# Running sums of the stick-breaking attention: softplus tiles of later key blocks added on VectorE, 768 ones columns a head in place of 1280

## The reference

```
z = einsum('bqhd,bshd->bhqs', qb, k) * HEAD_DIM ** -0.5
causal = pos[None, :] < t[:, None]
log_keep = where(causal, log_sigmoid(-z), 0.0)
after = cumsum(log_keep, axis=3, reverse=True) - log_keep
w = where(causal, exp(log_sigmoid(z) + after), 0.0)
out = einsum('bhqs,bshd->bqhd', w, v)
```

## Time and profile before

| | us |
|---|---|
| median of 3 runs | 1367.83 (1367.25 to 1368.55) |
| the profiled execution | 1367.21 |
| its span | 1365.5 |
| PE busy | 1264.2 (93%) |
| DVE busy | 804.4 (59%) |
| ACT busy | 437.7 (32%) |
| POOL busy | 158.8 (12%) |

### The profile page before, as it was taken

The page is one execution under the profiler, slowest core; times in us unless marked ns, Lnnn a source line. Parts: engine busy times, 40 slices in busy tenths (PEclk is TensorE's granted clock), DMA queues, the critical chain, the costliest instruction groups (busy, mean ns, idle before and its releaser), DMA issues.

```text
span 1365.5 us, 16163 instructions
## 1 busy us (share of the span) xinstructions
PE 1264.2 (93%) x6140; PEld 1026.9 (75%) x6140; DVE 804.4 (59%) x1108; ACT 437.7 (32%) x589; POOL 158.8 (12%) x172
## 2 busy tenths in 40 slices
PE   4548778899999999999999999999999999999999
PEld 4346676778888888888877988556878888888887
DVE  2988887756555555465627895775474343343442
ACT  1323214133123132141324224786243132231321
POOL 1700450220000000004200000111400000000022
PEclk9769857999999999999999999999999999999999
DMA  8234736636444444443131222000322323233211
GB/s 257 77 100 130 218 95 226 210 121 214 161 147 178 161 158 163 163 162 115 22 119 62 93 93 93 1 1 1 119 67 93 93 92 96 88 109 105 92 61 62
DMA packets 136912, 157.68 MB, mean 115 GB/s; under 512 B 24168, under 2 KB 117536, under 8 KB 136864
## 3 DMA queue, kind: packets, MB, share of 16 engines
q1 hardware_dynamic: 121808, 151.72, 34.6%
q10 hardware_dynamic: 14480, 3.74, 1.4%
q0 software_dynamic: 576, 1.57, 0.3%
HBM read 151.65 MB, written 4.19 MB: 114 GB/s over the span
## 4 chain that ended last, share of the span: by engine, by line
PE 78%; DVE 13%; DMA 4%; ACT 2%; ACTq 2%; issue 1%; POOL 0%; DVEq 0%; SPq 0%
PE psum L1536 77%; DMA ada_ring<-in_ada_w 3%; DVE ada_acc L1007 2%; DVE w_lo L1174 1%; DVE work L1191 1%; ACTq L696 1%; DVE bz L978 1%; PE psum L1540 1%; DVE h_lo L1203 1%; DVE work L978 1%; ACT w_hi L710 1%; ACT pT L930 1%; DVE s_t L978 1%; DMA u_scratch<-ub 1%; DVE bd L1148 0%
## 5 line engine op out<-in xcount | busy, mean ns | idle before, releaser
L1536 PE MATMUL psum<-h_hi,w_hi 128*128 128x512 f32 x880 | 346.9, 394 | 14.8 <-DVE w_lo L1174 8.0
L1536 PE MATMUL psum<-h_lo,w_hi 128*128 128x512 f32 x880 | 344.3, 391 | 0.0
L1536 PE MATMUL psum<-h_hi,w_lo 128*128 128x512 f32 x880 | 344.0, 391 | 0.0
L710 ACT ACTIVATE w_hi<-w_raw 128x2048 fp32r<-128x2048 f32 x92 | 174.8, 1900 | 345.9 <-PE psum L1536 309.9
L1174 DVE TENSOR_TENSOR w_lo<-w_raw,w_hi 128x2048 fp32r<-128x2048 f32 x92 | 214.0, 2326 | 107.0 <-ACT w_hi L710 106.5
L1536 PEld LDWEIGHTS psum<-h_hi,w_hi 128*128 128x128 f32 x880 | 165.5, 188 | 55.4 <-issue 14.1
L1536 PE MATMUL psum<-a_hi,w_hi 128*128 128x512 f32 x512 | 202.4, 395 | 0.0
L1536 PE MATMUL psum<-a_hi,w_lo 128*128 128x512 f32 x512 | 202.2, 395 | 0.0
L1536 PE MATMUL psum<-a_lo,w_hi 128*128 128x512 f32 x512 | 202.1, 395 | 0.0
L1536 PEld LDWEIGHTS psum<-h_hi,w_lo 128*128 128x128 f32 x880 | 165.4, 188 | 35.9
L1536 PEld LDWEIGHTS psum<-h_lo,w_hi 128*128 128x128 f32 x880 | 165.6, 188 | 34.9
(11 more groups left out here) (279 smaller groups left out, 1473.2 us busy)
## 6 DMA issues: line engine op xcount, KB each, us to landing
w_raw<-in_mlp_w SPq DMA_DIRECT2D x64, 1024.0 KB, 5.3
ada_l_ring<-in_ada_w SPq DMA_DIRECT2D x64, 384.0 KB, 6.2
ada_ring<-in_ada_w SPq DMA_DIRECT2D x40, 384.0 KB, 4.3
w_raw<-in_cd_w_in SPq DMA_DIRECT2D x14, 1024.0 KB, 5.2
ada_first<-in_ada_w SPq DMA_DIRECT2D x24, 384.0 KB, 3.8
w_raw<-in_ab_w_in SPq DMA_DIRECT2D x4, 1024.0 KB, 7.0
w_raw<-in_ab_w_out SPq DMA_DIRECT2D x4, 1024.0 KB, 7.3
w_raw<-in_cd_w_out SPq DMA_DIRECT2D x4, 1024.0 KB, 5.1
```

Of the source, the lines that this page charges most:

```text
L710: act.activation(w_hi[n % 2][:, :, 0:w], raw[n % 2][:, :, 0:w], ACT.Copy).then_inc(hi_ready, 1)
L1536: return nc.tensor.matmul(o, lhsT, rhs, start=start, stop=stop, **kw)
```

## The change

A second place for sums appears: later_a (256 columns) and later_b (128 columns). A new DVE function, later_sums, waits until POOL has masked the softplus tiles of a head and then computes with three additions of 128 columns: later_b = query block 3 of key blocks 2 and 3 added; later_a, first half = query block 2 of key blocks 1 and 2 added; later_a, second half = query block 3 of key block 1 added to later_b, for which it waits for the first addition. It raises later_ready twice a head. DVE runs it for head s - 1 at the end of score_rows(s), behind |z| of head s; for the last head directly behind softplus_sum.

stick_sums waits for later_ready as well, before its first matmul. Block j then takes a ones matmul of 128 columns from the first tile of block j + 1, and for the rest one ones matmul from later_a (256 columns, block 0) or later_b (128 columns, block 1). Ones columns: 384 + 256 + 128 = 768 a head. The order of the float32 additions changes, the sums are the same.

```diff
@@ -203,6 +203,9 @@
     z_sb.append(place("z_sb2", [P, W1], F32, offset=sumsq_at))
     sp_sb = [lay(at, f"sp_sb{i}", [P, W1]) for i in range(2)]
     pT = lay(at, "pT", [P, NB, L])
+    later_a = lay(at, "later_a", [P, 2 * P])
+    later_b = place("later_b", [P, P], F32, offset=sumsq_at + 4 * 10 * P)
+    assert sumsq_at + 4 * 11 * P <= arena
     assert at[0] <= nc.sbuf_usable_end, (at[0], nc.sbuf_usable_end)
 
     p_at = [0, P, 3 * P, 6 * P]
@@ -386,6 +389,7 @@
     z_soft = sem("z_soft")
     sp_diag = sem("sp_diag")
     sp_ready = sem("sp_ready")
+    later_ready = sem("later_ready")
     r_ps = sem("r_ps")
     r_used = sem("r_used")
     w_exp = sem("w_exp")
@@ -1446,6 +1450,18 @@
             dve.scalar_tensor_tensor(out=sp_sb[head % 2][:, :], in0=z_sb[head % 3][:, :], scalar=0.0,
                                      in1=sp_sb[head % 2][:, :], op0=ALU.max, op1=A).then_inc(sp_diag, 1)
 
+        def later_sums(head):
+
+            s_ = sp_sb[head % 2]
+            dve.wait_ge(sp_ready, NB * (head + 1))
+            last_pair = s_[:, z_at[2] + P:z_at[2] + 2 * P]
+            own(dve.tensor_tensor(later_b[:, :], last_pair, s_[:, z_at[3]:z_at[3] + P], A))
+            dve.tensor_tensor(later_a[:, 0:P], s_[:, z_at[1] + P:z_at[1] + 2 * P], s_[:, z_at[2]:z_at[2] + P], A)\
+               .then_inc(later_ready, 1)
+            settle()
+            dve.tensor_tensor(later_a[:, P:2 * P], s_[:, z_at[1] + 2 * P:z_at[1] + 3 * P], later_b[:, :], A)\
+               .then_inc(later_ready, 1)
+
         def score_rows(step):
             for n in range(NB):
                 i = NB - 1 - n
@@ -1465,6 +1481,8 @@
             dve.tensor_scalar(sp_sb[step % 2][:, :].bitcast(I32), z_sb[step % 3][:, :].bitcast(I32),
                               0x7fffffff, None, ALU.bitwise_and)\
                .then_inc(z_abs, 1)
+            if step >= 1:
+                later_sums(step - 1)
 
         def score_norms(step):
             dve.wait_ge(p_exp, NB * (step + 1))
@@ -1850,6 +1869,7 @@
         def stick_sums(pr):
             s_ = sp_sb[pr % 2]
             pe.wait_ge(sp_ready, NB * (pr + 1))
+            pe.wait_ge(later_ready, 2 * (pr + 1))
             for j in range(NB):
                 if j < 2:
                     pe.wait_ge(t_copied, NB * pr + j + 3)
@@ -1858,10 +1878,11 @@
                 o = bank[j % 2]
                 w = (NB - j) * P
                 last = mm(o[:, 0:w], tri[:, :], s_[:, z_at[j]:z_at[j] + w], True, j == NB - 1)
-                for j2 in range(j + 1, NB):
-                    w2 = (NB - j2) * P
-                    last = mm(o[:, w - w2:w], ones[:, :], s_[:, z_at[j2]:z_at[j2] + w2], False,
-                              j2 == NB - 1)
+                if j < NB - 1:
+                    last = mm(o[:, P:2 * P], ones[:, :], s_[:, z_at[j + 1]:z_at[j + 1] + P], False, j == 2)
+                if j < 2:
+                    later = later_b if j else later_a
+                    last = mm(o[:, 2 * P:w], ones[:, :], later[:, 0:w - 2 * P], False, True)
                 last.then_inc(r_ps, 1)
 
         def outputs(pr):

```

## The result

The changed kernel takes 1379.57 us (median of 5 runs, 1375.8 to 1382.49) against 1367.83 us (1365.89 to 1370.87): a ratio of 1.0085, 95% interval 1.007 to 1.010. It is 11.7 us slower. The forecast had the direction, a fall of the clock as the main cost, and +6.5 us; the time lies 0.6 us above the stated range. Heads are counted as first to eighth, and the six middle heads are the second to the seventh.

The account below looks back on a forecast made before the run. PE was taken as the bound now, DVE as setting the period after the change. First head +1.06, middle heads +1.8, eighth -0.87 gave +2.0; clock falls +4.5 made +6.5, 1374.3 us, range 1368.2 to 1379.0.

Parts of the forecast that it names:

- PE's columns: Sums on PE: 512 of 1280 ones columns fewer in each head, 0.87 us a head won.
- The additions and the wait: Middle heads: sums start 1.50 us after the absolute value starts; period 12.34 us against 12.04, +1.8 us over six heads.
- the sum without the clock: Whole stage: first head 1.06, middle heads 1.8, eighth head -0.87, together +2.0 us without new clock effects.
- The last head: Eighth head: additions hidden behind ScalarE's copy with 0.8 us to spare, so 0.87 us is won.
- The clock in the middle heads: Second to seventh head: longer idle time before the sums makes the granted clock fall in three of six, +4.5 us.
- The first head: First head: sums start 1.93 us later, less 0.87 for columns, with the same 1.02 us clock loss: +1.06 us.
- the +3.5: First head: cost in us if all 3.47 us of the new sums run at half speed; not the value taken.
- DVE's longer period: Six middle heads: the loop through DVE takes 12.34 us against 12.04, 0.30 a head, +1.8 us.
- Rival B: Middle heads: same period with the clock at full speed throughout, +2.0 us, 1369.8 us; chance 30%.
- Rival C: Sums: additions fit under ScalarE's copy, which still releases them; each head wins 0.87 us, -7.0 us, 1360.9; chance 10%.

Follow-up runs that it names:

- the columns alone: Kernel before with ones matmuls cut to 768 columns, no additions and no wait, so the sums leave tiles out: 1361.20 us, ratio 0.9960.
- the filled version: Changed kernel with two unused matmuls of 512 and 128 columns on PE ahead of its wait for later_a: 1369.97 us, ratio 1.0028.
- the old columns: Changed kernel with its additions and wait, but the 1280 ones columns of the kernel before: 1381.54 us, ratio 1.0113.
- the additions without the wait: Changed kernel whose additions run on DVE, but PE neither waits for nor reads them, so the sums leave tiles out: 1360.46 us, ratio 0.9954.

## Why the prediction was right in kind and wrong in size

- **PE's columns: right.** 0.87 us a head forecast; periods of 11.18 against 12.03 with the columns alone, 0.85.
- **The additions and the wait: right.** From the start of the absolute value to the sums 1.52 us (1.50); period at full clock 12.26 (12.34). All middle heads at full clock would lose 6 x 0.23 = 1.4 us (1.8). The filled version shows this part alone: 2.65 us over the stage, where the sum without the clock had 2.0.
- **The last head: right.** The additions ended 0.87 us ahead of the copy (0.8), and its sums took 3.48 us in place of 4.34, 0.86 won.
- **The clock in the middle heads: the step that failed.** "I take 1.5 us a time and three heads of six: +4.5." Measured, five heads took 5.07 to 5.18 us in place of 3.48: 8.3 us together, 1.66 a fall. So the number was 5 and the size near the upper end, 1.7. This term was 3.8 us short. I had taken the count by placing the new gap between two cases of the trace. The runs show that the gap's length gives no count: at 1.37 to 1.48 us it is five of six twice, and two of six with the old columns.
- **The first head: the same step in small.** "If the same 1.02 us is lost after the later start, +1.06 stands." It didn't stand: 2.62 us were lost against full clock (6.10 for 3.48). Counted from the first scores of the step, the sums started 2.51 us later (forecast 1.93) and the last block came 3.25 us later (forecast 1.06), near the +3.5 that the prediction had set aside for sums at half speed throughout. Some 0.5 us of this came ahead of the sums: DVE's third score row waited 0.83 us for PE's scores in place of 0.28, at the low clock too. How much of the 3.25 us is the change's stays open. Both executions of the changed kernel took 6.10 us here, but the additions without the wait took 5.54 and the columns alone 3.51 for the same matmuls, so one execution's first head was no measure to forecast from.
- **The sum.** 3.25 (first head) + 8.3 (five falls) - 0.86 (last head) leaves 1.7 of 12.36 us for DVE's longer period (forecast 1.8). Against the forecast's 6.5 us, 3.8 are missing in the falls of the middle heads and 2.2 in the first head. Some 10 of 12.4 us are the clock's: filling the gap took 9.71 us off the stage. Rival B, the same period at full clock, is what the filled version is: +2.9.
- Rival C, written off as "a regrouping that I don't see", was partly within reach by one place in DVE's queue: ahead of the absolute value the idle time is 0.74 us in place of 0.29. Its price of -7.0 us was not. C wanted the additions to begin by 869.5, and the masks that they read end at 869.82; two places earlier DVE waited 0.34 us for them.

The Trainium skill's remark that repeated short gaps between groups of matmuls can make the clock swing (TensorE: Matmul & The Clock Gate, "A second HAM failure mode: psum-queue depth-cycling") agrees with these runs: full clock in every middle head with gaps up to 0.75 us, falls in five of six, five of six and two of six with 1.37 to 1.48.

## What to carry to other kernels

Work moved from a busy engine to an idle one must still be ready in time: look in the trace for when the second engine's queue gets to it before the first asks for it, and put it ahead of whatever isn't urgent there. Where PE's idle time in a loop grows past what the trace shows it to bear at full clock, allow for a fall of the clock in most rounds; here it was two to five of six, at 1.5 to 1.7 us each. A cheap test is to fill the gap with unused matmuls: if more work makes the kernel faster, the clock was the cost.

## What the runs showed of the hardware

- A gap of 1.37 to 1.48 us before the sums went with a fall in five middle heads of six where a head at full clock took 12.3 us, and in two of six where it took 13.1. What else decides stays open; no run here separates it.
- A fall costs nearly the same in every head (1.50 to 1.70 us), in the shorter heads and in the longer ones.
- The first head, with nothing changed in front of its sums, ran them at a granted clock of 0.81 in the profile before, 1.00 with the columns alone and 0.63 with the additions without the wait; between the last two, with the same matmuls, that is 2.03 us. Such differences may be part of the spread of some 5 us between runs of one kernel; no run here shows it.
